# Bias rows of forget attention spread over the partitions by DMA instead of by TensorE and ACT

## The chip, the cores and the metric

The kernel runs on one core of a Trainium2 chip. The metric is the device time of one launch in microseconds (us); the times before are those of three runs. The engines are named as in the profile: PE is TensorE, with PEld for its weight loads, DVE is VectorE, ACT is ScalarE, POOL is GpSimd, and SP is the engine that only issues DMAs here.

## The reference

Four layers work on 512 tokens of width 1024: two of one kind, then two of another, each with an MLP at its end. The change lies in the second kind, whose layers mix four branches; the fourth is forget attention, eight heads of 64 in which every key carries a bias that grows with the forgetting between it and the query:

```
log_f = log_sigmoid(f_logit + b_f)
cumT  = cumsum(log_f, over tokens)            # one row of 512 per head
s = einsum("bqhd,bkhd->bhqk", q, k) * scale
s = s + cumT[query] - cumT[key]
p = masked_softmax(s, key_pos <= query_pos)
o = einsum("bhqk,bkhd->bqhd", p, v)
```

`cumT[query]` is the same for a whole row of the softmax and falls out of it. The kernel adds only `-cumT[key]`.

## The kernel before

**Weights.** All weights stream from HBM in units of 128x1024 float32 (512 KB). SP loads a unit into one of two buffers `w_raw` (L256) once POOL is done with the unit two before it. ACT makes its upper part `w_hi` (L232), POOL the rest `w_lo` (L279), both with three buffers, and PE multiplies each tile in three products per k (L335, L336, L337) into one of two banks `acc`, which DVE evacuates. An ordinary unit is 24 products.

**Mixing stages.** After each branch a stage "mix" forms gates and adds the branch. In the third one (mix2), between its first and second half, PE turns the values of forget attention (L776, 16 transposes), ACT copies them out (L784), and the first bias rows are spread.

**Forget attention.** `PairAttention` works on two heads (a = 0 and 1) at a time. A pass p is one pair of heads, of which there are four, and has four slots, one for each block of 128 queries; so there are slots s = 0 to 15. Scores of slot s are over 128, 256, 384 or 512 keys. Every engine runs its own list of slots in order:

- PE in slot s: the scores of slot s (L606, then the causal masks L613), at slots 6, 10 and 14 the values of the pass before (L655), the bias of the next pass where one is due, the turning of the probabilities of slot s-2 (L638), and then k-parts of the weight tiles of the group gate3 as filling (L335 to L337).
- ACT: the exponentials of slot s (L684), the bias copies (L699), the turned probabilities of slot s-2 out of PSUM (L708), weight splits (L232).
- DVE: scores plus bias with their extreme in one instruction (L739), for a = 0 and 1, then the normalising of slot s-1 (L759), then the evacuation of filled tiles.

Score number h = 2s + a goes to bank h % 3, so PE may begin it only once L739 has read number h - 3. The turned probabilities go through two banks in turn, numbered by n; PE may fill one only when ACT has copied number n - 2.

**The bias.** `small` holds in partition 64 + 2t + a the row `-cumT` of head a of pair t. `pe_bias` (L622) spreads one row over 128 partitions by a product of a column of the identity, repeated over 128 columns, with `small[64:96, :]`, into a turning bank; `act_bias` (L699) copies the bank to `extra`, which lies in `Z0[:, 8:12, :]` with two buffers for two passes. Pair 0 is made in mix2; `bias_due` places pair 1 at slot 2, pair 2 at slot 6 and pair 3 at slot 10. Below, "pair p" means the two bias rows of pass p.

Of the kernel before, what the change touches and what calls it, by code (L numbers as in the profile page):

```python
# [21 lines left out]
ACT = mybir.ActivationFunctionType  # L22
AX_X = mybir.AxisListType.X

P = 128
T = 512
# [78 lines left out]
def program(nc, given, out):  # L105
# [5 lines left out]
    with ctx:  # L111
# [89 lines left out]
        def up(s, n=1):  # L201


            total[s.num] = total.get(s.num, 0) + n
            return s

        def since(s):


            return begin.get(s.num, 0)  # L210
# [310 lines left out]
        class PairAttention:  # L521
# [6 lines left out]
            def __init__(self, sems_of, passes, P_sb, PT_sb, stat, gate, fill, extra=None, take_output=None, p_scaled=None):  # L528
                (self.s_ready, self.max_ready, self.exp_done, self.p_normed, self.pt_turned, self.pt_ready, self.pv_done,
                 self.o_free) = sems_of  # L530
                self.passes, self.P, self.PT, self.stat, self.gate = passes, P_sb, PT_sb, stat, gate
                self.extra, self.take_output, self.p_scaled = extra, take_output, p_scaled
                self.parts = NK * fill
                self.n = NT * len(passes)
                self.score_banks, self.turn_banks, self.out_bank = B[0:3], B[3:5], B[5]
# [19 lines left out]
            def turn_at(self, s, a):  # L555

                biases = 2 * min(s // NT + 2, len(self.passes)) if self.extra is not None else 0
                return 2 * s + a + biases

            @staticmethod  # L560
            def bias_at(p, a):

                return 10 * p - 8 + a if p else a

            def bias_due(self, slot):

                p = (slot + 2) // NT
                return p if self.extra is not None and (slot + 2) % NT == 0 and p < len(self.passes) else None
# [5 lines left out]
            def pe(self, other=None, side=None):  # L574
                for slot in range(self.n + 3):
                    if slot < self.n:
                        self.pe_scores(slot)
                    if self.values_due(slot) is not None:
                        self.pe_values(self.values_due(slot))
                    if self.bias_due(slot) is not None:  # L580
                        self.pe_bias(self.bias_due(slot))
                    if 2 <= slot < self.n + 2:
                        self.pe_turn(slot - 2)
                    if other:
                        todo = self.filled(slot + 1) - self.filled(slot)
                        while todo:
                            n = min(todo, NK - other.k)
                            other.part(n)
                            todo -= n
                    if side:  # L590
                        side(slot)
# [24 lines left out]

            def pe_bias(self, p):
                for a in range(2):
                    n = self.bias_at(p, a)
                    if n >= 2:  # L620
                        pe.wait_ge(self.pt_ready, since(self.pt_ready) + n - 1)
                    pe.matmul(self.turn_banks[n % 2][:, :], self.passes[p]["sel"][a], self.passes[p]["bias"],  # L622
                              start=True, stop=True).then_inc(up(self.pt_turned), 1)
# [69 lines left out]
            def act_bias(self, p):  # L693
                for a in range(2):
                    n = self.bias_at(p, a)
                    act.wait_ge(self.pt_turned, since(self.pt_turned) + n + 1)
                    if p >= 2:
                        act.wait_ge(self.max_ready, since(self.max_ready) + 2 * NT * (p - 1))
                    act.activation(self.extra[:, p % 2, a, :], self.turn_banks[n % 2][:, :], ACT.Copy).then_inc(up(self.pt_ready), 1)  # L699
# [30 lines left out]
            def dve_max(self, s, a):  # L730
# [4 lines left out]
                if self.passes[p]["kind"] == "fox":  # L735
                    dve.wait_ge(self.pt_ready, since(self.pt_ready) + self.bias_at(p, a) + 1)
# [788 lines left out]
        gate_opened_nsa, y_split = sem("gate_opened_nsa"), sem("y_split")  # L1525

        def second_layer(layer):
# [3 lines left out]
            with scope:  # L1531
# [61 lines left out]
                def split_pair(t, bank, free):  # L1593
                    link(dve, dve.tensor_copy(yH[:, t, :], bank[:, :]))
                    dve.tensor_tensor(yL[:, t, :], bank[:, :], yH[:, t, :], ALU.subtract).then_inc(up(free), 1)
                att = PairAttention(attention_sems[0], make_passes(nsa), probs, probsT, stat, gate, 6, take_output=split_pair)
                forget = [[dict(kind="fox", q=Z1[:, t, :], k=Z1[:, 4 + t, :],
                                v=lambda kt, a, t=t: turned1[8 + t][:, kt, HD * a:HD * a + HD],
                                sel=[ident[64:96, 64 + 2 * t + a:65 + 2 * t + a].to_broadcast([32, P]) for a in range(2)],
                                bias=small[64:96, :])] for t in range(4)]  # L1600
                fox = PairAttention(attention_sems[1], make_passes(forget), probs, probsT, stat, None, 8,
                                    extra=Z0[:, 8:12, :].rearrange("p (i a) t -> p i a t", a=2), take_output=split_pair)
# [98 lines left out]
                def on_tensor():  # L1701
# [156 lines left out]
                    pe.wait_ge(decay_summed, since(decay_summed) + 1)  # L1858
                    fox.pe_bias(0)
# [11 lines left out]
                def on_scalar():  # L1871
# [129 lines left out]
                    def forget_begins():  # L2001
                        turn_act([turned1[8 + t] for t in range(4)], 10)
                        fox.act_bias(0)
# [388 lines left out]
```

## Time and profile before

| | us |
|---|---|
| median of 3 runs | 3787.05 |
| lowest and highest run | 3785.53, 3789.91 |
| the profiled execution, its own time | 3788.32 |
| its span | 3787.0 |

The profile is one execution. "Busy" is the time that an engine's instructions cover. The chain of waits follows the work that ended last back from the end, from each instruction to what released it. The timeline lists instructions in order of time with the idle time before them in brackets and what ended it. Mean granted TensorE clock over the span was 0.977 of full speed, 2.4 GHz.

### The profile page before, as it was taken

The numbers are of one execution on the slowest core, as the hardware profiler recorded it, in microseconds if no ns is written. First come the engines' busy times: TensorE is split into PE (matmuls) and PEld (weight loads), VectorE is DVE, ScalarE is ACT, GpSimd is POOL, SyncE is SP. The second block draws the span as 40 slices with busy tenths as digits, with TensorE's granted clock in tenths as the row PEclk, the third lists the DMA queues.
The fourth block names the chain that finished last, engine by engine and source line by source line (L and its number), as shares of the span: only waits on it lengthen the run. The fifth ranks groups of instructions, "written<-read, shape, count | busy, mean of one in ns | idle before, by whom it ended". The sixth has DMA issues, their size and how long they took to land.

```text
span 3787.0 us, 44713 instructions
## 1 busy us (share of the span) xinstructions
PE 3647.9 (96%) x17876; PEld 2806.5 (74%) x17876; DVE 2129.4 (56%) x3000; ACT 1335.4 (35%) x2282; POOL 1194.9 (32%) x486
## 2 busy tenths in 40 slices
PE   8889999988999999999999999999999999999998
PEld 6656888865588888577777678887767777778887
DVE  7787565688754565533364585446553255365444
ACT  5355121444521231545323532122354433342212
POOL 0003444200144443132323244444213232334443
PEclk9889999998999999999999999999999999999999
DMA  4101333220133343121222133334112122223332
GB/s 133 45 12 56 95 100 95 89 68 12 34 95 96 99 135 86 35 73 56 78 62 78 51 91 99 95 95 150 48 40 78 57 79 60 70 70 95 99 95 84
DMA packets 80798, 292.39 MB, mean 77 GB/s; under 512 B 9648, under 2 KB 11088, under 8 KB 80080
## 3 DMA queue, kind: packets, MB, share of 16 engines
q1 hardware_dynamic: 77808, 278.49, 24.2%
q10 hardware_dynamic: 2784, 11.03, 0.9%
q8 instruction: 143, 2.34, 0.3%
q14 instruction: 63, 0.52, 0.0%
HBM read 285.30 MB, written 2.10 MB: 76 GB/s over the span
## 4 chain that ended last, share of the span: by engine, by line
PE 86%; DVE 10%; ACT 2%; issue 2%; DMA 0%; SPq 0%; DVEq 0%; ACTq 0%
PE acc L335 23%; PE acc L337 23%; PE acc L336 23%; PE banks L976 3%; PE banks L606 2%; PE banks L655 2%; PE banks L638 2%; DVE conv_c L1394 1%; PE banks L993 1%; PE banks L1727 1%; DVE stat L742 1%; DVE pair L407 1%; PE banks L613 1%; PE banks L1824 0%; DVE near L919 0%
## 5 line engine op out<-in xcount | busy, mean ns | idle before, releaser
L279 POOL TENSOR_TENSOR w_lo<-w_raw,w_hi 128x1024 fp32r<-128x1024 f32 x482 | 1194.7, 2479 | 2565.0 <-ACT w_hi L232 2565.0
L232 ACT ACTIVATE w_hi<-w_raw 128x1024 fp32r<-128x1024 f32 x518 | 549.0, 1060 | 1733.6 <-PE acc L337 1648.1
L335 PE MATMUL acc<-hH,w_hi 128*128 128x512 f32 x1776 | 731.4, 412 | 11.9 <-DVE sig L2115 6.6
L337 PE MATMUL acc<-hL,w_hi 128*128 128x512 f32 x1776 | 699.4, 394 | 0.0
L336 PE MATMUL acc<-hH,w_lo 128*128 128x512 f32 x1776 | 699.1, 394 | 0.0
L335 PEld LDWEIGHTS acc<-hH,w_hi 128*128 128x128 f32 x1776 | 338.1, 190 | 98.6 <-issue 26.6
L335 PE MATMUL acc<-H,w_hi 128*128 128x512 f32 x1024 | 400.4, 391 | 3.8 <-DVE L L399 3.8
L335 PE MATMUL acc<-midH,w_hi 128*128 128x512 f32 x1024 | 401.0, 392 | 0.2
L370 DVE TENSOR_TENSOR xT<-acc,xT 128x512 f32<-128x512 f32 x160 | 110.5, 691 | 513.6 <-PE acc L337 501.2
L336 PE MATMUL acc<-midH,w_lo 128*128 128x512 f32 x1024 | 398.7, 389 | 0.0
L337 PE MATMUL acc<-midL,w_hi 128*128 128x512 f32 x1024 | 398.6, 389 | 0.0
L336 PE MATMUL acc<-H,w_lo 128*128 128x512 f32 x1024 | 398.4, 389 | 0.0
L337 PE MATMUL acc<-L,w_hi 128*128 128x512 f32 x1024 | 398.4, 389 | 0.0
L337 PEld LDWEIGHTS acc<-hL,w_hi 128*128 128x128 f32 x1776 | 337.2, 190 | 73.8
L336 PEld LDWEIGHTS acc<-hH,w_lo 128*128 128x128 f32 x1776 | 338.3, 190 | 66.5 <-issue 4.3
L335 PEld LDWEIGHTS acc<-midH,w_hi 128*128 128x128 f32 x1024 | 192.2, 188 | 46.5 <-DVE midL L509 7.0
L335 PEld LDWEIGHTS acc<-H,w_hi 128*128 128x128 f32 x1024 | 192.2, 188 | 46.0 <-DVE L L399 5.5
L336 PEld LDWEIGHTS acc<-H,w_lo 128*128 128x128 f32 x1024 | 192.2, 188 | 40.7 <-issue 1.0
L337 PEld LDWEIGHTS acc<-midL,w_hi 128*128 128x128 f32 x1024 | 192.2, 188 | 40.4
L337 PEld LDWEIGHTS acc<-L,w_hi 128*128 128x128 f32 x1024 | 192.2, 188 | 40.0
L336 PEld LDWEIGHTS acc<-midH,w_lo 128*128 128x128 f32 x1024 | 192.2, 188 | 39.3
L508 DVE CAST midH<-relu_sb 128x512 fp32r<-128x512 f32 x64 | 160.3, 2504 | 2.2
(338 smaller groups left out, 4710.7 us busy)
## 6 DMA issues: line engine op xcount, KB each, us to landing
w_raw<-in_stream SPq DMA_DIRECT2D x518, 512.0 KB, 3.6
cw<-in_cmpw ACTq DMA_DIRECT2D x2, 2048.0 KB, 7.3
mixed<-in_cmpw ACTq DMA_DIRECT2D x2, 2048.0 KB, 12.9
x_tok<-in_x SPq DMA_DIRECT2D x2, 1024.0 KB, 7.3
out<-probsT SPq DMA_DIRECT2D x4, 512.0 KB, 4.0
stack<-Z ACTq DMA_DIRECT2D x8, 128.0 KB, 2.4
stack<-Z ACTq DMA_DIRECT2D x8, 127.8 KB, 2.5
masks_f<-in_masks SPq DMA_DIRECT2D x1, 960.0 KB, 11.8
```

The costliest lines, as they stand in the source:

```text
L232: act.activation(w_hi[:, u % WB, 0:w], w_raw[:, u % 2, 0:w], ACT.Copy).then_inc(hi_split, 1)
L279: pool.tensor_tensor(w_lo[:, u % WB, 0:w], w_raw[:, u % 2, 0:w], w_hi[:, u % WB, 0:w], ALU.subtract)\
L335: pe.matmul(acc[n % 2][:, :], wh, H[:, k, :], start=(k == 0), stop=False)
L336: pe.matmul(acc[n % 2][:, :], wl, H[:, k, :], start=False, stop=False)
L337: last = pe.matmul(acc[n % 2][:, :], wh, Lo[:, k, :], start=False, stop=(k == nk - 1))
L370: dve.tensor_tensor(xT[:, i, :], a[:, :], xT[:, i, :], ALU.add).then_inc(up(free), 1)
L407: dve.tensor_tensor(sq[:, 0, :], sq[:, 0, :], sq[:, 1, :], ALU.add).then_inc(sq_added, 1)
L508: link(dve, dve.tensor_copy(midH[:, i, :], r))
L606: last = pe.matmul(self.score_banks[h % 3][:, 0:m], w["q"][r, qt * P:(qt + 1) * P], w["k"][r, lo * P:hi * P], start=True, stop=True, skip_ ...
L638: last = pe.transpose(self.turn_banks[n % 2][:, j * P:(j + 1) * P], self.P[:, s % 3, a, j * P:(j + 1) * P], ident)
L655: pe.matmul(self.out_bank[HD * a:HD * a + HD, cols], w["v"](kt, a), self.PT[:, a, kt, cols], start=(first and kt == 0), stop=True, skip_gr ...
L976: last = pe.matmul(scores, KK[r, jt * P:(jt + 1) * P], moving, start=(j == 0), stop=True, skip_group_check=True)
```

## The change

The product and the ACT copy of the bias are gone. `act_bias` issues for each row a DMA from SBUF to SBUF on ACT's queue: source is the one row of `small`, read 128 times with a step of zero, destination the 128 partitions of `extra`. It counts on one of two new semaphores `extra_loaded`, one for each buffer, and DVE's L739 waits for both rows of its pass there instead of for the ACT copy. Pairs 0 and 1 are now issued together in mix2, where pair 0 was made; pairs 2 and 3 are issued at slots 6 and 10, where they were made. The turning banks are used by turned probabilities alone, and their numbering loses the biases.

```diff
             def turn_at(self, s, a):
-                biases = 2 * min(s // NT + 2, len(self.passes)) if self.extra is not None else 0
-                return 2 * s + a + biases
+                return 2 * s + a
             def bias_due(self, slot):
                 p = (slot + 2) // NT
-                return p if self.extra is not None and (slot + 2) % NT == 0 and p < len(self.passes) else None
+                return p if self.extra is not None and (slot + 2) % NT == 0 and 2 <= p < len(self.passes) else None
...
-            def pe_bias(self, p):
-                for a in range(2):
-                    n = self.bias_at(p, a)
-                    if n >= 2:
-                        pe.wait_ge(self.pt_ready, since(self.pt_ready) + n - 1)
-                    pe.matmul(self.turn_banks[n % 2][:, :], self.passes[p]["sel"][a], self.passes[p]["bias"],
-                              start=True, stop=True).then_inc(up(self.pt_turned), 1)
...
             def act_bias(self, p):
+                if p >= 2:
+                    act.wait_ge(self.max_ready, since(self.max_ready) + 2 * NT * (p - 1))
                 for a in range(2):
-                    n = self.bias_at(p, a)
-                    act.wait_ge(self.pt_turned, since(self.pt_turned) + n + 1)
-                    if p >= 2:
-                        act.wait_ge(self.max_ready, since(self.max_ready) + 2 * NT * (p - 1))
-                    act.activation(self.extra[:, p % 2, a, :], self.turn_banks[n % 2][:, :], ACT.Copy).then_inc(up(self.pt_ready), 1)
+                    act.dma_start(self.extra[:, p % 2, a, :], self.passes[p]["bias"][a]).then_inc(up(self.extra_loaded[p % 2], 16), 16)
...
-                    dve.wait_ge(self.pt_ready, since(self.pt_ready) + self.bias_at(p, a) + 1)
+                    dve.wait_ge(self.extra_loaded[p % 2], since(self.extra_loaded[p % 2]) + 32 * (p // 2 + 1))
...
+                def rows_of(x, row):
+                    one = x[row:row + 1, :]
+                    return bass.AP(one.tensor, one.offset, [one.ap[0], [0, P], [1, T]])
...
-                    pe.wait_ge(decay_summed, since(decay_summed) + 1)
-                    fox.pe_bias(0)
...
-                        fox.act_bias(0)
+                        act.wait_ge(decay_summed, since(decay_summed) + 1)
+                        for p in range(2):
+                            fox.act_bias(p)
```

PE in mix2 of the first such layer, where pair 0 was made. L776 turns the values, L335 begins the second half of mix2:

```order
7052 L776 MATMUL banks<-C,Z_1 128x128 x15
7053 L622 MATMUL banks<-small,C 128x512 [waits decay_summed]
7054 L622 MATMUL banks<-small,C 128x512
7055 L335 MATMUL acc<-yH,w_hi 128x512 [waits acc_free1,lo_split]
```

After the change the L622 rows are missing there, and L335 stands right behind L776.

PE at slot 10, before:

```order
7347 L655 MATMUL banks<-probsT_1,Z_1 64x128 x2
7348 L622 MATMUL banks<-small,C 128x512 [waits pt_ready_1] x2
7349 L638 MATMUL banks<-C,probs_1 128x128 [waits p_normed_1,pt_ready_1] x2
7350 L335 MATMUL acc<-hH,w_hi 128x512
```

and after, where lines 599, 606, 640 and 623 are what L606, L613, L655 and L638 were:

```order
7338 L599 MATMUL banks<-Z_1 128x384 [waits max_ready_1] x2
7339 L606 MATMUL banks<-Cb 128x128 x2
7340 L640 MATMUL banks<-probsT_1,Z_1 64x512 [waits pt_ready_1]
...
7344 L640 MATMUL banks<-probsT_1,Z_1 64x128 x2
7345 L623 MATMUL banks<-C,probs_1 128x128 [waits p_normed_1,pt_ready_1] x2
```

The turning follows on the values at once. ACT at the same slot, before and after (L669 and L691 were L684 and L708, and L682 is the new DMA):

```order
1058 L684 ACTIVATE probs_1,stat_1<-probs_1,stat_1 128x384 [waits pt_turned_1,max_ready_1] x2
1059 L699 ACTIVATE Z_1<-banks 128x512 [waits max_ready_1,pt_turned_1] x2
```

```order
1059 L669 ACTIVATE probs_1,stat_1<-probs_1,stat_1 128x384 [waits pt_turned_1,max_ready_1] x2
1060 L682 DMA Z_1<-small 128x1x512 [waits max_ready_1]
1061 L682 DMA Z_1<-small 128x1x512
1062 L691 ACTIVATE probsT_1<-banks 128x128 [waits pv_done_1,pt_turned_1] x2
1063 L669 ACTIVATE probs_1,stat_1<-probs_1,stat_1 128x512 [waits pt_turned_1,max_ready_1] x2
```

The two copies became two DMA issues in the same place, with no wait for PE. On DVE the order stays; L739 (now L722) waits for `extra_loaded` in place of `pt_ready`.

## Rows read from the trace of the kernel before

**Rows 1.** The page: busy time by engine, and the chain's shares by engine.

```profile
PE 3647.9 (96%) x17876; PEld 2806.5 (74%) x17876; DVE 2129.4 (56%) x3000; ACT 1335.4 (35%) x2282; POOL 1194.9 (32%) x486
PE 86%; DVE 10%; ACT 2%; issue 2%; DMA 0%; SPq 0%; DVEq 0%; ACTq 0%
```

**Rows 2.** View of one line, L622: shortest, median and longest in ns.

```profile
L622 PE MATMUL banks<-small,C x32: 587/587/691, 2029.1 to 3314.1; 32*128 32x512 f32 x32
```

**Rows 3.** Timeline of PE in mix2: start us, us, engine, line, instruction.

```profile
2029.06 1.98 PE L622 MATMUL banks<-small,C 32*128 32x512 f32 x4
...
2030.97 0.50 PE L335 MATMUL acc<-yH,w_hi 128*128 128x512 f32 x1
```

**Rows 4.** Timeline, slot 10, PE and ACT.

```profile
2126.35 0.19 ACT L684 ACTIVATION_READ_ACCUMULATOR probs<-probs,stat 128x1 f32 x1
2126.88 1.98 PE L622 MATMUL banks<-small,C 32*128 32x512 f32 x4
2128.04 0.60 ACT L699 ACTIVATE Z<-banks 128x512 f32<-128x512 f32 x1 [1.50 <-PE banks L622]
...
2129.63 0.48 PE L335 MATMUL acc<-hH,w_hi 128*128 128x512 f32 x1
```

**Rows 5.** Timeline of PE, slot 14, which has no bias.

```profile
2148.28 0.44 PE L638 MATMUL banks<-C,probs 128*128 128x128 f32 x2
2148.48 0.48 PE L335 MATMUL acc<-hH,w_hi 128*128 128x512 f32 x1
```

**Rows 6.** Timeline of PE, beginning of slots 0, 2 and 3.

```profile
2074.73 0.49 PE L606 MATMUL banks<-Z 64*128 64x128 f32 x4
...
2081.15 0.92 PE L606 MATMUL banks<-Z 64*128 64x384 f32 x4
...
2085.28 0.48 PE L335 MATMUL acc<-hH,w_hi 128*128 128x512 f32 x1
...
2088.20 1.13 PE L606 MATMUL banks<-Z 64*128 64x512 f32 x4
...
2089.75 0.47 PE L335 MATMUL acc<-hH,w_hi 128*128 128x512 f32 x1
```

**Rows 7.** Timeline, slot 12 on DVE and the beginning of slot 13 on PE.

```profile
2137.90 0.28 DVE L739 CUSTOM_DVE_ANT_0 probs<-banks,Z 128x128 f32<-128x128 f32 x1
...
2138.52 2.26 DVE L759 TENSOR_SCALAR probs<-probs,stat 128x512 f32<-128x512 f32 x2
...
2140.41 0.70 PE L606 MATMUL banks<-Z 64*128 64x256 f32 x4
```

**Rows 8.** DMA issues: count, KB each, median us from issue to landing.

```profile
w_raw<-in_stream SPq DMA_DIRECT2D x518, 512.0 KB, 3.6
cw<-in_cmpw ACTq DMA_DIRECT2D x2, 2048.0 KB, 7.3
...
stack<-Z ACTq DMA_DIRECT2D x8, 128.0 KB, 2.4
...
alpha<-in_alpha ACTq DMA_DIRECT2D x2, 16.0 KB, 1.8
```

**Rows 9.** View of one line, L1887: ns on ACT's queue for one issue.

```profile
L1887 ACTq DMA_DIRECT2D stack<-Z x8: 468/468/519, 1433.4 to 2639.6; - x8
```

**Rows 10.** PE after idle time: timeline, then stretches (after POOL: PEclk, DMA, GB/s).

```profile
2014.63 0.49 PE L335 MATMUL acc<-hH,w_hi 128*128 128x512 f32 x1 [3.31 <-DVE sig L2115]
...
2014.60:2018.40 3.80, 3.77 (x10) 2.97 (x11) 0.69 (x1) 2.26 (x3) 2.08 (x1) 0.55 0.00 0
...
2104.00:2111.00 7.00, 6.57 (x18) 4.09 (x18) 0.00 (x0) 1.64 (x4) 0.00 (x0) 0.76 0.22 70
```

**Rows 11.** Timeline of POOL and ACT in mix2: w_lo of two units, w_hi of the next.

```profile
2043.39 2.47 POOL L279 TENSOR_TENSOR w_lo<-w_raw,w_hi 128x1024 fp32r<-128x1024 f32 x1 [2.97 <-ACT w_hi L232]
...
2048.83 2.40 POOL L279 TENSOR_TENSOR w_lo<-w_raw,w_hi 128x1024 fp32r<-128x1024 f32 x1 [2.97 <-ACT w_hi L232]
...
2053.13 1.06 ACT L232 ACTIVATE w_hi<-w_raw 128x1024 fp32r<-128x1024 f32 x1 [3.76 <-PE acc L337]
```

More of the change, by code:

```diff
@@ L521, in program, with __init__ @@
         class PairAttention:
-            def __init__(self, sems_of, passes, P_sb, PT_sb, stat, gate, fill, extra=None, take_output=None, p_scaled=None):
+            def __init__(self, sems_of, passes, P_sb, PT_sb, stat, gate, fill, extra=None, take_output=None, p_scaled=None, extra_loaded=None):
                 (self.s_ready, self.max_ready, self.exp_done, self.p_normed, self.pt_turned, self.pt_ready, self.pv_done,
@@ L532, in __init__ @@
                 self.extra, self.take_output, self.p_scaled = extra, take_output, p_scaled
+                self.extra_loaded = extra_loaded
                 self.parts = NK * fill
@@ L555, in turn_at @@
             def turn_at(self, s, a):
-                biases = 2 * min(s // NT + 2, len(self.passes)) if self.extra is not None else 0
-                return 2 * s + a + biases
-            @staticmethod
-            def bias_at(p, a):
-                return 10 * p - 8 + a if p else a
+                return 2 * s + a
             def bias_due(self, slot):
                 p = (slot + 2) // NT
-                return p if self.extra is not None and (slot + 2) % NT == 0 and p < len(self.passes) else None
+                return p if self.extra is not None and (slot + 2) % NT == 0 and 2 <= p < len(self.passes) else None
             def values_due(self, slot):
@@ L579, in pe @@
                         self.pe_values(self.values_due(slot))
-                    if self.bias_due(slot) is not None:
-                        self.pe_bias(self.bias_due(slot))
                     if 2 <= slot < self.n + 2:
@@ L1525, in program @@
         gate_opened_nsa, y_split = sem("gate_opened_nsa"), sem("y_split")
+        extra_loaded = [sem(f"extra_loaded{i}") for i in range(2)]
         def second_layer(layer):
@@ L1596, in second_layer @@
                 att = PairAttention(attention_sems[0], make_passes(nsa), probs, probsT, stat, gate, 6, take_output=split_pair)
+                def rows_of(x, row):
+                    one = x[row:row + 1, :]
+                    return bass.AP(one.tensor, one.offset, [one.ap[0], [0, P], [1, T]])
                 forget = [[dict(kind="fox", q=Z1[:, t, :], k=Z1[:, 4 + t, :],
                                 v=lambda kt, a, t=t: turned1[8 + t][:, kt, HD * a:HD * a + HD],
-                                sel=[ident[64:96, 64 + 2 * t + a:65 + 2 * t + a].to_broadcast([32, P]) for a in range(2)],
-                                bias=small[64:96, :])] for t in range(4)]
+                                bias=[rows_of(small, 64 + 2 * t + a) for a in range(2)])] for t in range(4)]
                 fox = PairAttention(attention_sems[1], make_passes(forget), probs, probsT, stat, None, 8,
-                                    extra=Z0[:, 8:12, :].rearrange("p (i a) t -> p i a t", a=2), take_output=split_pair)
+                                    extra=Z0[:, 8:12, :].rearrange("p (i a) t -> p i a t", a=2), take_output=split_pair, extra_loaded=extra_loaded)
                 rec = Recurrence(1, [BB[:, r:r + 1] for r in range(2)], gap, QK, near, SS, refs, [(5 * NK, 10)] * 2)
```

## The prediction

> **What bounds the kernel now.** I read the page first. TensorE (PE) is busy 96% of the span and carries 86% of the chain of work that ended last [rows 1], so what is taken from PE in its own order shortens the kernel nearly one for one, and what is taken from ACT, DVE or POOL is worth nothing unless PE waits for it. Then I read the timeline at the places where the bias rows are spread. The row of the L622 products has 32 records, two for each of 16 products: four pairs (p = 0 to 3) in each of two layers [rows 2]. The places look alike in both layers, so I work out one layer, the first, and double it.
>
> **What is removed, pair by pair.** Pair 0 stands after the 16 transposes of L776 in the third mixing stage. Its products start at 2029.06 us, and the next weight product at 2030.97 us [rows 3]. PE has nothing else in between and waits for nothing, so 1.91 us go.
>
> Pairs 2 and 3 stand at slots 6 and 10 of forget attention, behind the values (L655). At slot 10 the products start at 2126.88 us. The turning products (L638) that follow need the two turning banks, which ACT empties only after the biases: the first copy of a bias ends at 2128.64 us, the second some 0.9 us later, and PE takes up its weight products at 2129.63 us [rows 4]. From the start of L622 to there are 2.75 us. Slot 14 is the same slot without a bias: L638 starts at 2148.28 us and the weight product at 2148.48 us, 0.20 us [rows 5]. So a late pair costs PE 2.55 us, the products and the wait for the copies together.
>
> Pair 1 stands at slot 2. From the first score to the first weight product are 2085.28 - 2081.15 = 4.13 us. Slot 3, which has no bias, needs 2089.75 - 2088.20 = 1.55 us with wider scores and two transposes more [rows 6]. The scores of slot 2 take 0.21 us less (0.92 against 1.13), and I take 0.20 us off for the two transposes, by rows 5: 1.15 us. The pair costs 2.98 us.
>
> The sum is 1.91 + 2.98 + 2.55 + 2.55 = 10.0 us a layer, 20.0 us in both. The 16 ACT copies go as well, but ACT is idle around them (before the first it sat idle for 1.50 us) [rows 4], so beyond the waits counted they bring nothing.
>
> **What is added.** Each layer gets eight copies by DMA from one row of `small` to 128 partitions, 256 KB written each. Issuing one took ACT's queue 0.47 us for the nearest row, the SBUF to SBUF copy into `stack` [rows 9]. Two are 0.9 us where two copies of 0.60 us went. The four at the start are 1.9 us on an engine that then has only the next weight split to do, which waits for PE's tile. I cost the issues at nothing; L708, the first work queued behind the late ones, feeds values that PE needs only slots later.
>
> The landing is the question. The bounds come from the DMA issues. The 16 KB load took 1.8 us, which I take as the fixed part, the copy into `stack` (128 KB, 64 partitions to 64) 2.4 us, and a weight load of 512 KB 3.6 us [rows 8]. By these a pair of copies, 512 KB, would land in 3.6 to 4.2 us (the latter at the 0.6 us beyond the fixed part for each 128 KB). But in every one of these rows many partitions give or take the bytes. Here all 512 KB are read out of two neighbouring partitions. The fastest row is the load into `cw`: 2048 KB in 7.3 us, or 5.5 us beyond the fixed part, 372 KB/us over 128 partitions and 16 engines [rows 8]. That is 23.3 KB/us for each sixteenth, eight partitions. No row shows a sixteenth of SBUF moving more. If the source is held to that, a copy takes 256 / 23.3 = 11.0 us, and a pair 1.8 + 22.0 = 23.8 us. Held to what one partition took in that row, 16 KB in 5.5 us, a pair would take 178 us, which I keep only as the far end. I take 23.8 us: a single source row is nearer to one sixteenth than to all of them, and nothing says that one partition alone is worse than eight.
>
> The Trainium skill, SBUF — State Buffer, section "Door 1: The DMA port swizzle", speaks against this change: DMA bandwidth depends on how many of 16 ports the partitions reach, at about 27.2 GB/s for each, and partitions 64 to 67 lie on one port, 68 to 71 on another. By it, as an estimate, a pair would take some 21 us instead of 23.8 us, and the forecast would be some 11 us lower. No row of this trace has a source so narrow.
>
> **When the rows are needed.** Pairs 0 and 1 are asked for at about 2031 us. Four copies end by 2031 + 1.8 + 44 = 2077 us, the first two by 2055 us. Slot 0 begins at 2074.73 us in before, and pair 1 isn't needed until slot 4, which comes after slot 3 at 2088.20 us [rows 6]. Both are hidden.
>
> Pairs 2 and 3 have only two slots. At slot 10 ACT has finished its exponentials at 2126.54 us [rows 4] and issues. DVE needs the row at slot 12, at 2137.90 us in before [rows 7], 2.55 us earlier after: 8.8 us after the issue. What DVE holds back there: its score minimum L739, then the normalising of slot 11 (L759), the evacuation of the weight tiles, and through L739 the second score of slot 13 on PE, which needs the bank of slot 12's first one. That score goes out 0.3 us after L606 starts at 2140.41 us [rows 7], so 2138.16 us after the change, 11.6 us after the issue. With landing at 2126.54 + 23.8 = 2150.3 us and 0.3 us of L739 before it, PE stands still for 12.4 us. L759 of slot 11, 2.26 us for two [rows 7], is then late for L638: I take 1.0 us. After an idle time of 3.31 us before 2014.63 us PE ran at a granted clock of 0.55, near the 1.2 GHz level, through 10 products in 3.8 us [rows 10], where an ordinary unit of 24 products takes 5.44 us, the distance of two w_lo in mix2 [rows 11], 0.227 us each: 1.5 us lost. So a late pair costs 12.4 + 1.0 + 1.5 = 14.9 us, and the four of them 59.6 us.
>
> **The sum.** 59.6 - 20.0 = +39.6 us. On the span of 3787.0 us it is 3826.6 us; the profiled execution took 3788.3 us, 1.3 us beyond its span and within the scatter of the runs around their median of 3787.05 us. I forecast **3827 us**.
>
> **Rivals.** First, the copies land as fast as wide ones. The point from which the wait decides is a pair of 11 us; below it nothing is late, and the 20.0 us are all gain: 3767 us. For it speaks that a copy is cut over all engines like any other and that 128 KB between partitions took only 2.4 us [rows 8]; against it, the single source. Slot 6 ran at a granted clock of 0.76 right after its waits [rows 10]; where a dip goes with the waits, another 1 to 2 us a layer come on top. With a pair at 16 us, four waits of 5 us just eat the gain: about 3787 us. That is the dead middle.
>
> Second, the copies are slow and also hold the weight loads, since both use the same 16 engines. This one ends on the slow side. Its place is the mixing stage after pair 0. There a w_raw buffer is free when POOL ends at 2045.86 us, and the unit's split on ACT is at 2053.13 us [rows 11], 7.3 us for a load, with about as much more until PE needs it. If every engine alternates between a weight row of 4 KB and a bias row of 2 KB, four weight units move in the 44 us of the four copies, where PE eats one in 5.44 us. PE then loses 44 - 22 - 7 = 15 us a layer, 30 us in all: 3857 us. It decides as soon as a load takes over 14 us.
>
> Third, the far end: one partition gives less than a sixteenth did. At half the rate each late pair costs 22 us more: 3915 us.
>
> **How the numbers follow.** The forecast, slow copies and weights unharmed, gets 0.43, with its own range 3805 to 3845 us (a pair in 18 to 28 us). Fast copies get 0.30, 3762 to 3772 us. Slow copies with starved weights get 0.16, the middle (a pair in 11 to 18 us) 0.07, the far end 0.04. The range of **3762 to 3857 us** holds the first two, the middle and half of the third. A measurement of this kernel can tell about 0.2%, 7.6 us. Faster: fast copies and a part of the middle, 0.32. Same: 0.05. Slower: 0.63. So sign and size hang on one duration that the trace doesn't hold.
>
> **What would show it.** In the profile after, the time from issue to landing of the copies from `small`: about 13 us for the first and 24 us for a pair asked for together if I am right, 3 to 5 us if the first rival is. In the slow case L739 waits for a DMA four times for some 12 us, at slots 8 and 12 of each layer, and L606 behind it. Either way PE goes from L776 straight to the weight product, and slots 2, 6 and 10 are shorter by 3.0, 2.6 and 2.6 us. Starved weights would show as L232 waiting for w_raw in the mixing stage. Wrong would also be a gain below 20 us with no wait anywhere: then the products had filled time that PE spends otherwise.

## The result, and the profile after

| | before, us | after, us |
|---|---|---|
| median | 3787.24 (5 runs) | 3854.27 (5 runs) |
| lowest and highest | 3785.53, 3789.91 | 3850.46, 3855.65 |
| span of the profiled execution | 3787.0 | 3851.5 |

The change makes the kernel slower: the ratio is 1.0173, interval 1.0161 to 1.0184, some 67 us. It lies inside the range, 2.7 us below its upper end, and 27 us above the forecast. The mean granted TensorE clock was 0.969, against 0.977 before.

The page after, its parts that answer to [rows 1] and [rows 8]:

```profile
PE 3650.4 (95%) x17844; PEld 2816.0 (73%) x17844; DVE 2124.9 (55%) x3000; ACT 1326.5 (34%) x2266; POOL 1195.2 (31%) x486
...
PE 81%; DVE 10%; DMA 3%; issue 2%; ACT 2%; ACTq 1%; POOL 0%; SPq 0%; DVEq 0%
...
Z<-small ACTq DMA_DIRECT2D x16, 256.0 KB, 20.4
```

PE has 32 instructions less and is busy 2.5 us longer. DMA, 0% of the chain before, now carries 3% of it, and ACT's DMA queue 1% instead of 0%. The new copies land in 20.4 us (median).

The view of the line of the new copies, L682 (shortest, median and longest; the three numbers of the first row are ns on the issuing queue):

```profile
L682 ACTq DMA_DIRECT2D Z<-small x16: 477/618/9560, 2026.3 to 3368.1; - x16
...
  DVE probs L722: 45.3, 4
...
DMA to landing us min/median/max: 11.8/20.4/32.4
```

The first copy of a group lands in 11.8 to 12.0 us, the second of a late pair in some 20.5 us. L722 on DVE (L739 before) waits for them four times, 45.3 us in all. And one issue held ACT's queue for 9.56 us, where the nearest row of before had 0.47 us.

**A late pair.** Timeline of PE around slot 9 (first layer), which answers to [rows 7]:

```profile
2125.59 0.70 PE L599 MATMUL banks<-Z 64*128 64x256 f32 x2
2134.95 1.22 PE L599 MATMUL banks<-Z 64*128 64x256 f32 x2 [8.66 <-DVE stat L722]
2136.10 0.40 PE L606 MATMUL banks<-Cb 128*128 128x128 bf16 x2
2136.28 1.95 PE L623 MATMUL banks<-C,probs 128*128 128x128 f32 x8
2137.89 0.78 PE L335 MATMUL acc<-hH,w_hi 128*128 128x512 f32 x1
```

Here PE stands still for 8.66 us between two scores of one slot. The copies had been issued at 2113.46 and 2113.99 us, and L722 started at 2134.59 us. Then PE runs at the lower level of 1.2 GHz: L335 takes 0.78 us, where slot 14 of before had 0.48 us [rows 5]. The stretches after the wait say how long (columns as below):

```profile
2135.00:2141.40 6.40, 6.40 (x20) 4.98 (x21) 3.12 (x13) 4.60 (x13) 1.43 (x1) 0.50 0.03 11
2141.80:2150.00 8.20, 8.20 (x44) 4.47 (x42) 1.74 (x7) 1.75 (x6) 0.55 (x1) 1.00 0.67 79
```

The granted clock is 0.50 for 6.4 us behind an idle time of 8.66 us, and 1.00 after that.

**The mix stage.** Timeline of ACT and its DMA queue in mix2, which answers to [rows 11]:

```profile
2026.34 0.55 ACTq L682 DMA_DIRECT2D Z<-small  x1
...
2026.93 0.62 ACTq L682 DMA_DIRECT2D Z<-small  x1
...
2027.58 6.77 ACTq L682 DMA_DIRECT2D Z<-small  x1
...
2034.37 9.56 ACTq L682 DMA_DIRECT2D Z<-small  x1
2044.04 1.06 ACT L232 ACTIVATE w_hi<-w_raw 128x1024 fp32r<-128x1024 f32 x1 [15.77 <-issue]
2048.32 1.06 ACT L232 ACTIVATE w_hi<-w_raw 128x1024 fp32r<-128x1024 f32 x1 [3.23 <-DMA w_raw<-in_stream]
2067.00 1.06 ACT L232 ACTIVATE w_hi<-w_raw 128x1024 fp32r<-128x1024 f32 x1 [17.62 <-DMA w_raw<-in_stream]
```

Two things happen. The third and fourth issue don't leave ACT's queue for 16.3 us, and the weight split L232 stands behind them for 15.77 us, although its weight unit had landed at 2026.3 us (issued at 2022.8 us, 3.5 us). Later L232 waits another 17.62 us for a weight load. PE stands still twice (timeline of PE):

```profile
2047.56 0.79 PE L335 MATMUL acc<-hH,w_hi 128*128 128x512 f32 x1 [4.93 <-POOL w_lo L279]
2070.54 0.80 PE L335 MATMUL acc<-hH,w_hi 128*128 128x512 f32 x1 [9.35 <-POOL w_lo L279]
```

The first wait belongs to the split behind the held issues, the second to the late load. Together they are 14.3 us, and 4.89 and 9.38 us in the second layer. Right behind the two waits the granted clock was 0.51 and 0.59 (2047.5 to 2053 us and 2070.5 to 2074 us). One L335 there follows the other after 1.28 us instead of 0.68 us, which by my estimate from these rows cost some 4 us more.

Weight loads of this kernel take 3.3 us at least and 3.6 us in the median. The view of their line, L256, for 2026.5 to 2050 us has the two that were issued beside the copies:

```profile
L256 SPq DMA_DIRECT2D w_raw<-in_stream x2: 327/328/328, 2028.2 to 2047.5; - x2
...
DMA to landing us min/median/max: 19.4/19.8/20.1
```

Stretches of the mix stage show how that comes about (after POOL: granted clock, DMA share, GB/s):

```profile
2028.30:2034.30 6.00, 6.00 (x28) 4.96 (x27) 2.77 (x4) 0.00 (x0) 0.00 (x0) 1.00 0.90 27
2036.00:2038.00 2.00, 2.00 (x11) 1.65 (x10) 0.74 (x2) 0.00 (x0) 0.00 (x0) 1.00 0.91 28
2038.20:2046.00 7.80, 4.43 (x20) 3.34 (x18) 1.14 (x2) 1.06 (x1) 0.83 (x1) 1.00 1.00 78
2048.20:2057.80 9.60, 9.60 (x34) 7.71 (x33) 0.69 (x1) 1.06 (x1) 2.37 (x1) 0.76 0.89 27
2058.00:2065.00 7.00, 3.19 (x15) 2.30 (x13) 0.69 (x1) 0.00 (x0) 0.00 (x0) 1.00 0.98 77
```

While the first copy runs, the 16 DMA engines are busy 90% of the time and move 27 GB/s, the pace of the copies, although a weight load has been waiting since 2028.2 us. The total rises only when the first copy has landed, at 2038.1 us: then it is 78 GB/s, and the load lands with the second copy at 2048.3 us. The load issued at 2047.5 us fares the same: 27 GB/s until the third copy has landed, 77 GB/s beside the fourth. So a load of 20 us here is about 10 us in which it doesn't advance and 10 us in which it shares the engines with a slow copy. In the second part 78 - 27 = 51 GB/s of weights go beside 27 GB/s of bias rows, two to one, which fits engines that alternate one 4 KB weight row with one 2 KB bias row; the alternation itself is inferred. At slot 9 a load issued at 2125.3 us landed after 10.4 us: the total was 27 GB/s from 2126 to 2133 us and 203 GB/s from 2134 to 2136 us, when the second copy had landed.

**Where the 67 us went.** I compared the places of both layers, from the first score of one slot to that of the next, and the mix stage from the first L335 after the place of pair 0 to slot 0:

| place | before, us | after, us | difference, us |
|---|---|---|---|
| pair 0's products, each layer | 1.91 | 0 | -1.91 |
| mix2 to slot 0, layers 1, 2 | 43.76, 43.76 | 62.36, 63.84 | +18.6, +20.1 |
| slot 2 | 7.05, 7.05 | 4.07, 4.06 | -3.0, -3.0 |
| slots 6 and 10, layer 1 | 10.63, 9.05 | 6.47, 6.49 | -4.2, -2.6 |
| slots 6 and 10, layer 2 | 9.05, 10.64 | 6.47, 6.49 | -2.6, -4.2 |
| slots 9 and 13, layer 1 | 4.48, 4.50 | 16.95, 16.55 | +12.5, +12.1 |
| slots 9 and 13, layer 2 | 4.50, 4.50 | 16.18, 16.25 | +11.7, +11.8 |

Gains -23.2, late pairs +48.0, mix stage +38.7: +63.5 us, against 64.5 us between the two spans. The rest is small only in sum: after the change the first of these places comes 3.0 us earlier, the stretch between the layers is 3.2 us longer and the end 0.9 us longer. The change touches nothing there, and no run shows why. Over the traces of all runs below the first place begins anywhere between 2022.9 and 2030.4 us, so a difference of a few us between two kernels isn't shown to come from the edit unless the places themselves show it.

### The profile page after: what moved, and what is told of

The parts are those of the page before. It is cut to its first block, busy times and chain, and to the rows that moved or that the text cites. A ratio compares the mean times of both kernels' runs of the same rounds, so it can differ in the third digit from the quotient of the medians.

```text
span 3851.5 us, 44637 instructions
## 1 busy us (share of the span) xinstructions
PE 3650.4 (95%) x17844; PEld 2816.0 (73%) x17844; DVE 2124.9 (55%) x3000; ACT 1326.5 (34%) x2266; POOL 1195.2 (31%) x486
## 4 chain that ended last, share of the span: by engine, by line
PE 81%; DVE 10%; DMA 3%; issue 2%; ACT 2%; ACTq 1%; POOL 0%; SPq 0%; DVEq 0%
PE acc L335 22%; PE acc L336 21%; PE acc L337 21%; PE banks L959 3%; PE banks L599 2%; DMA Z<-small 2%; PE banks L640 2%; PE banks L623 2%; DVE conv_c L1377 1%; DMA w_raw<-in_stream 1%; PE banks L976 1%; DVE stat L725 1%; PE banks L1713 1%; ACTq L682 1%; DVE w_lo L248 1%
## 5 line engine op out<-in xcount | busy, mean ns | idle before, releaser
L232 ACT ACTIVATE w_hi<-w_raw 128x1024 fp32r<-128x1024 f32 x518 | 548.9, 1060 | 1770.9 <-PE acc L337 1606.6
L335 PE MATMUL acc<-hH,w_hi 128*128 128x512 f32 x1776 | 737.7, 415 | 40.4 <-POOL w_lo L279 28.6
L335 PEld LDWEIGHTS acc<-hH,w_hi 128*128 128x128 f32 x1776 | 341.3, 192 | 129.7 <-POOL w_lo L279 30.2
L335 PE MATMUL acc<-H,w_hi 128*128 128x512 f32 x1024 | 400.4, 391 | 3.8 <-DVE L L399 3.8
L335 PE MATMUL acc<-midH,w_hi 128*128 128x512 f32 x1024 | 401.0, 392 | 0.3
L335 PEld LDWEIGHTS acc<-midH,w_hi 128*128 128x128 f32 x1024 | 192.2, 188 | 46.4 <-DVE midL L509 7.0
L335 PEld LDWEIGHTS acc<-H,w_hi 128*128 128x128 f32 x1024 | 192.2, 188 | 46.1 <-DVE L L399 5.5
L599 PE MATMUL banks<-Z 64*128 64x512 f32 (+3 forms) x512 | 146.6, 545 | 43.9 <-DVE stat L722 34.2
## 6 DMA issues: line engine op xcount, KB each, us to landing
mixed<-in_cmpw ACTq DMA_DIRECT2D x2, 2048.0 KB, 12.8
Z<-small ACTq DMA_DIRECT2D x16, 256.0 KB, 20.4
```

Source lines behind the costliest of these rows:

```text
L232: act.activation(w_hi[:, u % WB, 0:w], w_raw[:, u % 2, 0:w], ACT.Copy).then_inc(hi_split, 1)
L335: pe.matmul(acc[n % 2][:, :], wh, H[:, k, :], start=(k == 0), stop=False)
L599: last = pe.matmul(self.score_banks[h % 3][:, 0:m], w["q"][r, qt * P:(qt + 1) * P], w["k"][r, lo * P:hi * P], start=True, stop=True, skip_ ...
```

## The experiments

My theory after this was: a source in few partitions reads slowly; that alone makes both losses; each place costs what the table says, and the edits of PE's order are a gain of 20 to 23 us. The rivals were that 128 times one row is slow for another reason (that the same bytes are read again), that the copies lose time whatever their source because they are DMAs, and that the losses in the mix stage come from something else in the change.

### e1_wide: the same copies from 128 partitions

```diff
-                                bias=[rows_of(small, 64 + 2 * t + a) for a in range(2)])] for t in range(4)]
+                                bias=[cosT[:, :] for a in range(2)])] for t in range(4)]
```

> The changed kernel with one difference: each of the 16 copies reads a whole tile of 128 partitions (cosT) instead of one row of small read 128 times. Bytes, destinations, issues and waits are the same; the bias added is not the right one. Theory (the single source row is what is slow): the copies land in 3 to 5 us, DVE never waits for them, ACT's queue is not held by an issue, and all that is left is the gain of 20 us and the clock dips of 3 us, 3764 to 3768 us. Rival (it is the number of bytes or the issue of eight more copies on ACT's queue, whatever they read): landing stays near 20 us, 3850 us.

Measured 3767.73 us, ratio to before 0.9944, interval 0.9929 to 0.9959. The line of the copies:

```profile
L682 ACTq DMA_DIRECT2D Z<-cosT x16: 492/618/633, 2030.0 to 3295.1; - x16
...
DMA to landing us min/median/max: 2.3/5.2/5.8
```

Number, size, queue and places of the copies are those of the change, and all is gone: no issue over 0.63 us, no wait at L722, landing in 5.2 us. So the source makes all of the loss, and the kernel without products and ACT copies is 20.6 us faster than the before of the same session (3788.35 us). By places its trace gains 23.4 us; 3.0 us of that are lost again ahead of, between and behind them, where the edit changes nothing.

### e6_four_near and e7_four_far: four source rows, on one port or on four

Both read four partitions of `cosT`, each 32 times; near are 64 to 67, far are 64, 68, 72 and 76.

```diff
-                    return bass.AP(one.tensor, one.offset, [one.ap[0], [0, P], [1, T]])
+                    return bass.AP(one.tensor, one.offset, [[4 * one.ap[0][0], 4], [0, P // 4], [1, T]])
```

This is the far one; near has 1 for the first 4. In both the source row is `rows_of(cosT, 64)`.

> The changed kernel with the source of every copy widened from one row to four rows in the neighbouring partitions 64 to 67 of cosT, each read 32 times; bytes, destinations, issues and waits are the same, and the bias added is not the right one. In the changed kernel a lone copy landed after 11.8 us and the second of a pair 8.7 to 9.3 us behind it. Theory (the limit belongs to a group of partitions, a port, as the Trainium skill has it in SBUF, State Buffer, section Door 1, and 64 to 67 share one): no faster, first copy 11 to 13 us, pair 20 to 22 us, 3845 to 3860 us. Rival (the limit belongs to the single partition): four partitions give four times as much, a copy in 4 to 5 us, 3764 to 3770 us.

> As the run before, but the four rows lie in partitions 64, 68, 72 and 76 of cosT. Theory (a port serves 64 to 67 together and others serve the rest): four groups give four times as much, a copy in 4 to 5 us, a pair in 6 to 7 us, nothing is late, 3764 to 3770 us. Rival (the four source rows only cut the copy over four DMA engines, and that is what sets its time): the same as with neighbouring rows, whatever that is.

Measured 3852.86 us near and 3760.92 us far, one run each. A stretch of near in which only the copies move:

```profile
2126.00:2132.00 6.00, 0.00 (x0) 0.00 (x0) 0.00 (x0) 0.00 (x0) 0.00 (x0) 0.53 0.23 26
```

and two of far, behind the load and the issues of the same slot:

```profile
2097.00:2099.00 2.00, 2.00 (x15) 1.74 (x14) 1.71 (x6) 1.01 (x3) 0.00 (x0) 1.00 0.26 96
2099.00:2101.00 2.00, 2.00 (x14) 1.35 (x13) 1.97 (x5) 2.00 (x5) 0.00 (x0) 1.00 0.25 94
```

26 GB/s against 94 to 96 GB/s from the same number of source partitions. Four near rows are as slow as one row (3852.86 us against 3854.27 us), so it is not the single partition, and the far rows are read as often as the near ones, so it is not the repeated reading. Nor is it the number of DMA engines that the copy is cut over: the share is 0.23 near and 0.25 to 0.26 far. The Trainium skill, SBUF — State Buffer, "Door 1: The DMA port swizzle", says that 64 to 67 lie on one port and the far four on four, with some 27.2 GB/s each. The traces agree with that rule: one port gave 26 to 28 GB/s, four gave 3.6 times that. On DVE near waits 13.09 us and far 0.91 us for a late pair:

```profile
2132.83 0.29 DVE L722 CUSTOM_DVE_ANT_0 probs<-banks,Z 128x128 f32<-128x128 f32 x1 [13.09 <-DMA Z<-cosT]
```

```profile
2102.26 0.29 DVE L722 CUSTOM_DVE_ANT_0 probs<-banks,Z 128x128 f32<-128x128 f32 x1 [0.91 <-DMA Z<-cosT]
```

That far lies 7 us under e1_wide I don't count as a finding: it is one run, and the copies in mix2 start at 2023.2 us against 2030.0 us, so those 7 us arose ahead of the change's places; the places themselves are as long as in e1_wide.

### e9_late_narrow: only the late pairs from one row

```diff
-                                bias=[rows_of(small, 64 + 2 * t + a) for a in range(2)])] for t in range(4)]
+                                bias=[rows_of(small, 64 + 2 * t + a) if t >= 2 else cosT[:, :] for a in range(2)])] for t in range(4)]
```

> The changed kernel, but in each layer the copies of pairs 0 and 1, which lie in the mix stage, read the wide source cosT (128 partitions, one row each) and only those of pairs 2 and 3 read the narrow rows of small. What it leaves out: the bias of pairs 0 and 1 is not the right one. It measures the term of the late pairs alone. Theory: with all copies wide the kernel took 3767.7 us; each of the four late pairs costs what its place grew by in the changed kernel (12.5 and 12.1 us), while the mix stage is undisturbed: 3767.7 + 4 x 12.3 = about 3817 us, 3810 to 3823, with waits of 8 to 9 us on the copy at L722 in four places. Rival: the late waits were long only because the layer had been pushed by the disturbed mix stage, or part of them is given back later: under 3803 us.

Measured 3814.34 us, 1.0068, interval 1.0051 to 1.0085. Timeline of PE at slot 9:

```profile
2108.15 0.70 PE L599 MATMUL banks<-Z 64*128 64x256 f32 x2
2117.47 1.22 PE L599 MATMUL banks<-Z 64*128 64x256 f32 x2 [8.63 <-DVE stat L722]
```

Against e1_wide the four late pairs cost 46.6 us, 11.7 us each; in the first layer slots 9 and 13 took 16.15 and 16.09 us. The wait is the same as with a disturbed mix stage ahead of it (8.63 against 8.66 us), so the late pairs cost what they cost without that stage, and the rest, 3854.3 - 3814.3 = 40 us, is that of the mix stage. In the second layer the second issue at slot 10 was held for 6.97 us. Slot 11 then took 6.98 us instead of 4.5 us and slot 13 13.79 us, with the same sum.

### e8_beside: the kernel before with four idle copies in its mix stage

The four copies go from rows of `small` into tiles that are free there, and nothing reads them; DVE waits for them before slot 0 only so that the tiles can be used again. Products, ACT copies and all orders are those of before.

```diff
+                        act.wait_ge(decay_summed, since(decay_summed) + 1)
+                        for i in range(4):
+                            one = small[64 + i:65 + i, :]
+                            act.dma_start((probs[:, 2, i, :] if i < 2 else probsT[:, 0, i - 2, :]), bass.AP(one.tensor, one.offset, [one.ap[0], [0, P], [1, T]]))\
+                                .then_inc(up(spare_loaded[i], 16), 16)
```

> The kernel before, bias rows by TensorE and ACT and all, with four copies of one row of small to 128 partitions added behind pair 0 in the third mixing stage of each layer, into tiles that are free there; nothing reads what they bring, and DVE waits for them only ahead of slot 0. It prices the copies by what they do to others. Theory (held ACT queue and stretched weight loads cost the stretch up to slot 0 18.6 us a layer in the changed kernel, without anyone needing the rows there): third and fourth issue hold ACT's queue for 7 and 10 us again, and the kernel takes 3787 + 2 x 18 = 3823 us, between 3818 and 3830 us. Rival (the stretch grew because PE reached the weights earlier, with the 1.9 us of products gone and other changes around it): under 3800 us.

Measured 3832.61 us, 1.0121, interval 1.0104 to 1.0138, 2.6 us above the expected range. ACT in mix2:

```profile
2033.60 16.50 ACTq L2008 DMA_DIRECT2D probsT<-small  x2
2050.21 2.00 ACT L232 ACTIVATE w_hi<-w_raw 128x1024 fp32r<-128x1024 f32 x2 [16.85 <-issue]
2073.02 1.06 ACT L232 ACTIVATE w_hi<-w_raw 128x1024 fp32r<-128x1024 f32 x1 [20.81 <-DMA w_raw<-in_stream]
```

The copies, which nobody needs, cost 45.7 us by themselves against the before of the same session (3786.94 us): the same held issues (16.5 us), the same late load. The stretch to slot 0 took 62.95 and 63.52 us, 19.2 and 19.8 us more than before, 39.0 us in both layers. The two profiled executions differ by 43.5 us. Of the rest 1.2 us lie in slot 2 of the first layer, 1.3 us ahead of the first place and 1.9 us behind the last slot. So 39 us are the loss of the mix stage without anything else of the change.

### e2_split: pair 1 at the end of the mix stage

```diff
-                        for p in range(2):
-                            fox.act_bias(p)
-                    mix(2, forget_begins, lambda: None)
+                        fox.act_bias(0)
+                    mix(2, forget_begins, lambda: fox.act_bias(1))
```

> The changed kernel with pair 1 issued at the end of the third mixing stage instead of right behind pair 0, so that never more than two copies are queued. In the trace of the changed kernel the third and fourth issue held ACT's queue for 6.8 and 9.6 us, and the stretch from pair 0 to slot 0 grew by 18.6 us a layer. Theory (the loss there comes from ACT's queue being held, so that w_hi is late, together with a weight load that four queued copies stretch to 20 us): with two copies at a time the issue of the second is short, the stretch grows by under 5 us, and the kernel comes to 3820 to 3828 us. Rival (slow copies starve the weight loads for as long as they run, however they are grouped): the same 37 us of copying costs the same, 3848 to 3856 us.

Measured 3841.02 us, 1.0138, interval 1.0123 to 1.0153: between the two expectations, so both were wrong. The two issues ahead of mix2 are not held in either layer, and the stretch to slot 0 grows by 3.3 us instead of 18.6 us in the first layer and by 6.1 us instead of 20.1 us in the second. The load beside them still took 19.4 us, and PE waited 3.12 us for it. But the pair now collides with the loads of slot 2. ACT and PE there:

```profile
2088.50 1.06 ACT L232 ACTIVATE w_hi<-w_raw 128x1024 fp32r<-128x1024 f32 x1 [17.01 <-DMA w_raw<-in_stream]
```

```profile
2092.12 0.69 PE L623 MATMUL banks<-C,probs 128*128 128x128 f32 x2 [8.86 <-DVE probs L742]
```

ACT waits 17.01 us for a weight tile in the middle of attention, and the exponentials queued behind that wait keep DVE and PE idle for 8.86 us; slot 2 took 15.12 us instead of 4.07 us (13.33 us in the second layer). Two copies fewer in one place gave back 15 us there and cost 11 us in the next one. At slot 10 of the second layer one issue was held for 7.69 us.

### e3_early: pairs 2 and 3 two slots earlier

```diff
-                p = (slot + 2) // NT
-                return p if self.extra is not None and (slot + 2) % NT == 0 and 2 <= p < len(self.passes) else None
+                p = slot // NT + 1
+                return p if self.extra is not None and slot % NT == 0 and 2 <= p < len(self.passes) else None
```

> The changed kernel with pairs 2 and 3 issued at slots 4 and 8, as soon as their buffer has been read, instead of at slots 6 and 10. From the issue to the second score of slot 9 are then some 20 us instead of 12, and a pair lands in 21 us. Theory (the late pairs cost what is missing between landing and need, 12.3 us each with the slow clock behind it): at most 2 us of waiting and no clock dip are left at each of the four places, 3854 - 4 x 11 = 3810 us, between 3806 and 3818 us. Rival (the copies slow the weight loads beside them, so that what is saved in waiting comes back as PE waiting for weights): 3830 us or more.

Measured 3816.15 us, 1.0076, interval 1.0061 to 1.0091, in the expected range. Of the 45.3 us that L722 waited 8.9 us are left, and slots 9 and 13 took 4.5 to 9.0 us instead of 16.2 to 17.0 us, so not all of them came under the expected 2 us. Something new came in the first layer, on ACT at slot 4, and with it on PE at slot 5:

```profile
2104.12 6.79 ACTq L682 DMA_DIRECT2D Z<-small  x1
2110.97 0.87 ACT L691 ACTIVATE probsT<-banks 128x384 f32<-128x384 f32 x2 [6.69 <-issue]
```

```profile
2111.51 1.97 PE L623 MATMUL banks<-C,probs 128*128 128x128 f32 x8 [4.84 <-ACT probsT L691]
```

The second issue is held for 6.79 us, L691 stands behind it, and PE waits 4.84 us; slot 5 took 11.14 us instead of 4.5 us. In the second layer the same issue took 0.62 us and slot 5 was undisturbed.

### e4_both: both shifts

The two diffs above together. Pairs 2 and 3 go two slots earlier, as in e3_early, not four as the expectation says.

> Both shifts together: pair 1's copies are issued at the end of the second mix stage instead of ahead of it, and those of pairs 2 and 3 four slots earlier. Theory, additive: 3854.3 - 13.2 (pair 1 later) - 38.1 (pairs 2 and 3 earlier) = about 3803 us, 3798 to 3811, still slower than the kernel before, because every copy still takes 9 to 12 us from one row and stretches the weight loads beside it. Rival: the shifted copies meet more weight loads or held issues than each did alone, 3815 us or more. Second rival: with the waits gone the gains of the bias products come through whole, under 3790 us.

Measured 3809.45 us, 1.0053, interval 1.0038 to 1.0068: the upper end of the additive expectation. Both collisions came along: slot 2 took 14.16 us, and slot 5 took 11.34 us in the first layer. The best placing that I tried leaves this kernel 20 us slower than before. In every placing a pair, 512 KB, took some 20 us, with the share of the 16 engines at 0.9 while nothing else moved.

### e5_hbm: the row by way of HBM

The eight rows go to HBM once, 16 KB, before mix1, and the copies read them from there, each row 128 times, in the places of the changed kernel.

```diff
+                    act.wait_ge(decay_summed, since(decay_summed) + 1)
+                    act.dma_start(decays[layer - DEPTH], small[64:72, :]).then_inc(up(decays_stored, 16), 16)
...
-                                bias=[rows_of(small, 64 + 2 * t + a) for a in range(2)])] for t in range(4)]
+                                bias=[decays[layer - DEPTH, 2 * t + a:2 * t + a + 1, :].to_broadcast([P, T]) for a in range(2)])]
+                          for t in range(4)]
```

> The changed kernel with the rows taken through HBM: one store of the eight rows (16 KB) ahead of the second mixing stage, and each copy then reads its row of 2 KB from HBM 128 times. Places and waits of the copies as in the changed kernel. Theory (a source in one SBUF partition is slow, reading one row of HBM many times is not): a copy lands in 3 to 4 us, a pair in about 5 us, 3764 to 3768 us, faster than before. Rival (any source of 2 KB read 128 times is slow): 3850 us as the changed kernel.

Measured 3766.18 us, 0.9940, interval 0.9923 to 0.9957. This version computes everything and beats both kernels, the one before by 22 us in the same session. Its line of copies:

```profile
L682 ACTq DMA_DIRECT2D Z<-decays x16: 326/450/455, 2030.0 to 3295.0; - x16
...
DMA to landing us min/median/max: 3.0/4.2/6.5
```

One row of HBM read 128 times lands in 4.2 us; one row of SBUF read 128 times in 11.8 us at best.

## Why the prediction was near, and what it missed

**The outcome is not the forecast's own case.** The forecast, slow copies with weights unharmed, had its own range of 3805 to 3845 us and a chance of 0.43. What came is the second rival, slow copies with starved weights, which had 0.16. The measured time lies inside the whole range because that rival's 3857 us was its upper end.

**The products' gain held.** Worked out 20.0 us; by places it is 23.2 us in the two traces, because one low-clock dip a layer, about 1.6 us, went with the waits at slots 6 or 10. The text had named this and put no price into the sum. That e1_wide as a whole came out at 20.6 us is in part luck: its places gained 23.4 us too, and 3.0 us were lost where nothing was changed.

**The landing was the right bound, slightly too slow.** The step "a sixteenth of SBUF gives 23.3 KB/us" led to 23.8 us for a pair; 21.1 us were measured from the first issue to L722. The row of `cw` only showed what a sixteenth had given there, and a narrow source gives 26 to 28. The estimate of some 21 us, worked out from the figure for each port in the Trainium skill (SBUF — State Buffer, "Door 1: The DMA port swizzle"), was the better number.

**The late pair's term was mis-sized.** 14.9 us were forecast, 12.4 of them as wait. In the table a late pair costs 12.0 us on average. 8.40 to 8.66 us of it are wait, and some 3.4 us go to the low clock and what else is late, for which 2.5 us had been forecast; by e9_late_narrow it costs 11.7 us. The wait is shorter because the landing is 2.7 us quicker and because PE asks for the row 12.8 us after the issue, not 11.6 us. Over four pairs the sum was 11.6 us too high.

**"Both are hidden" was the step that failed.** It asked only when the rows of pairs 0 and 1 are needed, and rightly: nobody waited for them. What it left to the second rival is what they do to others. That rival named the place and half of the mechanism, engines that alternate 4 KB and 2 KB rows, with 15 us a layer; 18.6 and 20.1 us were measured. Its decision point was a load of 14 us, and loads took 19.4 and 20.1 us. But by alternation alone 512 KB at 51 GB/s would take some 10 us. The other 10 us, in which the load didn't advance beside a copy that was already running, and the held issues stood in no part of the working. The rival counted four loads in the time of the four copies; in the 40 us from the first issue to the last landing two landed. So its 15 us came near by another way than its own. The forecast had set this rival beside itself as an alternative, although both follow from the same slow copy: if the copies are slow, the engines are busy for all of that time. Given slow copies the second follows, as e8_beside shows, and their joint time should have been the forecast.

**"I cost the issues at nothing" was wrong as well.** The estimate of 1.9 us for four became 17.5 us on ACT's queue, and the first late w_hi of the mix stage hangs on it (15.77 us, idle time put down to the issue), and with it PE's first wait of 4.93 us, since the weights of that tile were there. No row of before shows an issue held. How the rest of the 18.6 us divides isn't settled. The load that PE's second wait of 9.35 us hangs on could be issued only at 2047.5 us, when POOL was done with the tile that the held issues had delayed, and then it was slow. e2_split has slow loads (19.4 us) without a held issue and grows by 3.3 and 6.1 us at this place, but with two copies instead of four.

**The sum, corrected:** 39.6 - 11.6 (late pairs) + 38.7 (mix stage) - 3.2 (clock dips) = 63.5 us, against 64.5 us between the spans. So the forecast was near partly by luck: a term too high by 11.6 us covered part of a term of 38.7 us that was left out.

**What would show it** came nearly as written. A first copy landed in 11.8 us (about 13 were expected) and a pair in 21.1 us (24). L739, now L722, waited at four places for 11.3 us on average (some 12), L335 came directly behind the transposes, and slots 2, 6 and 10 were shorter by 3.0, 2.6 and 2.6 us, with 1.6 us more once a layer. L232 waiting for w_raw was the sign of the second rival, and it came too.

Still open: why an issue is sometimes held with only one other copy queued (6.79 and 7.16 us at slot 4 in e3_early and e4_both, 7.69 and 6.97 us at slot 10 in e2_split and e9_late_narrow, each in one layer of two) while the same pair at slot 6 of the changed kernel goes out in 0.50 and 0.62 us. SP's issues of weight loads are touched too: the longest took 0.50 us before, 1.87 us in the changed kernel and 3.71 us in e8_beside. I found no rule for it in the traces, and ran nothing to find one. Open is also why a weight load doesn't advance beside a copy that is already running.

## What to carry to other kernels

Before a DMA replaces a product that spreads one row, look at which partitions its source touches: out of one row of SBUF 128 copies kept all 16 engines busy for nine to ten microseconds for 256 KB, and a weight load issued beside them took up to 20.1 us instead of 3.6 us. Price a slow transfer twice, once for who waits for it and once for who shares engines and issuing queue with it; the second can be the larger even where nobody waits for the transfer itself. If the row can make a short trip through HBM ahead of time, the same broadcast is cheap (4.2 us, and the whole kernel 22 us faster than before).

## What the runs showed of the hardware that I had not expected

- **A held DMA issue.** An issue that normally takes 0.47 to 0.62 us stood on ACT's queue for 6.77 and 9.56 us in the same places of both layers, as the third and fourth of four slow copies, and everything behind it in ACT's order stood too.
- **A load that stands beside a running copy.** While one slow copy ran, a weight load of another queue didn't advance for some 10 us (27 GB/s in total, the pace of the copy), and went on only when that copy had landed.
- **DMA share is not throughput.** With one source row the 16 engines read 0.90 busy at 27 GB/s; with four near rows the share read 0.23 at 26 GB/s.
- **Small source, other memory.** The same broadcast with the same number and size of writes took 11.8 us or more from one SBUF row and 4.2 us (median) from one HBM row.
